# Three query transposes of a two-layer hybrid attention trunk: from TensorE to 32x32 squares on VectorE and SBUF-to-SBUF transfers

## What is computed

```python
h = rms_norm(x, pre_w)
dq, dk, dv, dg, sq, sk, sv, sg, iq, ik, iw = split(h @ w_in)
dq, dk = rope(dq), rope(dk)                    # 4 heads x 2 maps x 64
oa = diff_attention(dq, dk, dv, lam)           # scale 64 ** -0.5
sq, sk = rope(sq), rope(sk)                    # 4 heads x 128
iq, ik = rope(iq), rope(layer_norm(ik))        # 8 index heads x 64
score = sum_h relu(iq_h @ ik.T) * iw_h         # the 64 best keys of each query are kept
ob = softmax over kept keys(sq @ sk.T * 128 ** -0.5) @ sv
y = concat(rms_norm(oa) * silu(dg), ob * silu(sg)) @ w_out
x = x + rms_norm(y, post_w)
```

## Time and profile before

| | us |
|---|---|
| median of three runs | 312.75 (311.55 to 312.98) |
| profiled execution, whole | 313.99 |
| its span, first to last instruction | 312.2 |
| PE busy in the span | 302.6 (97%) |
| DVE busy | 237.6 (76%) |
| ACT busy | 164.7 (53%) |
| POOL busy | 69.4 (22%) |
| packets of the hardware DMA queue, share of 16 engines | 48.2% |

### The profile page before, as it was taken

One profiled execution on the slowest core, in us unless ns is written; L12 is line 12 of the kernel. 1 busy time (PEld: TensorE's weight loads), 2 busy tenths in 40 slices (PEclk: granted clock), 3 DMA queues, 4 the chain that ended last, 5 costly groups with the idle time before them and its releaser, 6 DMA issues.

```text
span 312.2 us, 4324 instructions
## 1 busy us (share of the span) xinstructions
PE 302.6 (97%) x1564; PEld 250.2 (80%) x1564; DVE 237.6 (76%) x483; ACT 164.7 (53%) x284; POOL 69.4 (22%) x107
## 2 busy tenths in 40 slices
PE   8889999999999999999999999999999999999992
PEld 7668887787887888888888888778878788888881
DVE  4663979699999996883995178969999999679243
ACT  4678844736576275601775375463747635561100
POOL 1278910025030501101051301003413050110001
PEclk9999999999999999999999999999999999999998
DMA  7999969234514358134038576834452326300011
GB/s 233 361 346 351 364 230 327 81 133 146 198 61 138 121 190 316 49 133 134 0 112 290 171 242 260 278 129 134 134 161 110 135 71 205 129 2 0 0 67 67
DMA packets 27556, 51.61 MB, mean 165 GB/s; under 512 B 3344, under 2 KB 3600, under 8 KB 27536
## 3 DMA queue, kind: packets, MB, share of 16 engines
q1 hardware_dynamic: 27536, 51.34, 48.2%
HBM read 50.29 MB, written 1.05 MB: 164 GB/s over the span
## 4 chain that ended last, share of the span: by engine, by line
PE 91%; DMA 4%; SPq 2%; DVE 1%; ACT 1%; issue 0%; DVEq 0%; POOLq 0%; POOL 0%; ACTq 0%
PE bank_a L380 19%; PE bank_a L389 19%; PE bank_a L385 19%; PE bank_a L534 7%; PE bank_s L534 7%; PE bank_t L359 6%; DMA w_raw<-in_w_in 4%; PE bank_o L514 3%; PE bank_a L457 2%; PE bank_s L497 2%; PE bank_s L489 1%; PE bank_s L477 1%; PE bank_s L389 1%; PE bank_s L380 1%; PE bank_s L385 1%; SPq L283 1%
## 5 line engine op out<-in xcount | busy, mean ns | idle before, releaser
L870 DVE TENSOR_TENSOR w_lo<-w_raw,w_hi 128x2048 fp32r<-128x2048 f32 (+1 forms) x46 | 99.2, 2164 | 23.3 <-ACT w_hi L669 23.2
L669 ACT ACTIVATE w_hi<-w_raw 128x2048 fp32r<-128x2048 f32 (+1 forms) x46 | 82.0, 1785 | 39.8 <-PE bank_a L389 34.3
L380 PE MATMUL bank_a<-w_hi,h_hi 128*128 128x512 f32 x256 | 72.1, 403 | 0.0
L389 PE MATMUL bank_a<-w_lo,h_hi 128*128 128x512 f32 x256 | 68.8, 390 | 0.0
L385 PE MATMUL bank_a<-w_hi,h_lo 128*128 128x512 f32 x256 | 68.6, 390 | 0.0
L385 PEld LDWEIGHTS bank_a<-w_hi,h_lo 128*128 128x128 f32 x256 | 48.1, 188 | 10.4
L389 PEld LDWEIGHTS bank_a<-w_lo,h_hi 128*128 128x128 f32 x256 | 47.9, 188 | 10.5 <-DVE w_lo L870 0.5
L380 PEld LDWEIGHTS bank_a<-w_hi,h_hi 128*128 128x128 f32 x256 | 45.5, 188 | 10.2 <-issue 2.6
L1272 POOL TENSOR_TENSOR rt<-nat,tab 128x256 f32<-128x256 f32 x10 | 7.4, 736 | 110.7 <-ACT nat L714 110.6
L730 ACT ACTIVATE xt_pbuf<-xt_pbuf,st 128x128 f32<-128x128 f32 (+1 forms) x48 | 21.3, 445 | 12.7 <-DVE st L997 12.4
L714 ACT ACTIVATE nat<-bank_a,st 128x512 f32<-128x512 f32 x20 | 13.7, 684 | 23.3 <-PE bank_a L389 22.1
(11 more groups left out here) (174 smaller groups left out, 447.0 us busy)
## 6 DMA issues: line engine op xcount, KB each, us to landing
w_raw<-in_w_in SPq DMA_DIRECT2D x34, 1024.0 KB, 5.2
w_raw<-in_w_out SPq DMA_DIRECT2D x8, 1024.0 KB, 5.1
w_raw<-in_w_in SPq DMA_DIRECT2D x4, 512.0 KB, 6.7
prm<-in_rows SPq DMA_DIRECT2D x2, 705.0 KB, 8.9
xres<-in_x SPq DMA_DIRECT2D x2, 512.0 KB, 13.2
out<-xres SPq DMA_DIRECT2D x4, 256.0 KB, 2.1
xt_pbuf<-in_x_t SPq DMA_DIRECT2D x3, 256.0 KB, 6.3
w_raw<-in_w_in SPq DMA_DIRECT2D x4, 144.0 KB, 6.3
```

The source lines that it names most:

```text
L380: pe.matmul(bank, h_hi[:, HALF * half + kk, tok], whi[:, kk, :], start=half == 0 and kk == 0, stop=False)
L389: mm = pe.matmul(bank, h_hi[:, HALF * half + kk, tok], wlo[:, kk, :], start=False, stop=half == 1 and kk == HALF - 1)
L669: act.activation(unit(w_hi, u), unit(raw, u), ACT.Copy).then_inc(hi_done.sem, 1)
L870: dve.tensor_tensor(unit(w_lo, u), unit(raw, u), unit(w_hi, u).bitcast(F32), ALU.subtract).then_inc(lo_done.sem, 1)
```

## The change

`turn_nat` is no longer called for IQ, DQ and SQ; it stays for DK and SK. In its place:

- DVE turns all of a `nat` slot (both blocks, 128x1024) into 32x32 squares, each transposed in its own place, in one instruction that writes `mixn` (called `squares`).
- SP moves the squares: for each pair (i, j) of four row and four column groups one transfer from partitions 32i to 32i+31 to partitions 32j to 32j+31, of 32x8x32 float32, so 16 transfers of 32 KB in runs of 128 bytes. They are written into SP's program behind the load that follows `split_lo` of units 7, 12 and 15, after a wait for `squares_done`.
- PE waits for `iq_landed`, `dq_landed`, `sq_landed` before the score matmuls. DVE waits for the earlier spread before it writes `squares` again.
- DVE's drains for the three go. The scales of DQ and SQ, which the drains applied, move into ACT's `move`: POOL computes two more scaled copies of `rx` for each block (`rd`, `rs`).
- The layout of `iqT`, `dqT`, `sqT` is by block, then by 128-column group. The uses of the T banks fall from 25 to 19.

```diff
+SPREAD_BEHIND = (7, 12, 15)
+            def spread(dst, landed):
+                for i in range(SQUARES):
+                    for j in range(SQUARES):
+                        src = squares[i * LANES:(i + 1) * LANES, :].rearrange("p (a j r) -> p a j r", j=SQUARES, r=LANES)[:, :, j, :]
+                        to = dst[j * LANES:(j + 1) * LANES, :, :, i * LANES:(i + 1) * LANES].rearrange("p b f r -> p (b f) r")
+                        sp.dma_start(to, src).then_inc(landed.sem, 16)
...
+                    if u == SPREAD_BEHIND[0]:
+                        sp.wait_ge(squares_done.sem, squares_done.at(layer, 1))
+                        spread(iqT, iq_landed)
...
                 second(6)
-                turn_nat(T_IQ, 0, 1)
                 first(7)
...
                 pe.wait_ge(t_drained.sem, t_drained.at(layer, T_IK + 1))
+                pe.wait_ge(iq_landed.sem, iq_landed.at(layer, iq_landed.per_layer))
                 index_logits(0, 0, range(4))
...
                 first(11)
-                turn_nat(T_DQ, 1, 2)
                 second(11)
...
                 second(14)
-                turn_nat(T_SQ, 1, 4)
                 first(15)
...
+                    if chunk in (DQ, SQ):
+                        act.wait_ge(rq_ready.sem, rq_ready.at(layer, b + 1))
+                    if chunk in (DK, SQ):
+                        act.wait_ge(squares_done.sem, squares_done.at(layer, 1 if chunk == DK else 2))
+                    root = {DQ: rd, SQ: rs}.get(chunk, rx)
...
+                def turn_squares(slot, rope):
+                    dve.wait_ge(rope_done.sem, rope_done.at(layer, rope))
+                    if rope == 2:
+                        dve.wait_ge(iq_landed.sem, iq_landed.at(layer, iq_landed.per_layer))
+                    if rope == 4:
+                        dve.wait_ge(dq_landed.sem, dq_landed.at(layer, dq_landed.per_layer))
+                    dve.transpose(squares, nat[:, slot, :, :].rearrange("p b n -> p (b n)")).then_inc(squares_done.sem, 1)
...
                 split_lo(layer, 7)
+                turn_squares(0, 1)
                 split_lo(layer, 8)
                 index_key()
-                drain_pair(T_IQ, iqT)
...
                 choose(0, 4)
+                turn_squares(1, 2)
                 split_lo(layer, 13)
                 choose(0, 4)
                 mask_unchosen(0)
-                drain_pair(T_DQ, dqT, DIFF_QK ** -0.5)
...
+                turn_squares(1, 4)
                 split_lo(layer, 16)
-                drain_pair(T_SQ, sqT, E ** -0.5)
...
+                pool.wait_ge(rx_ready.sem, rx_ready.at(layer, b + 1))
+                pool.tensor_scalar(rd[:, b:b + 1], rx[:, b:b + 1], DIFF_QK ** -0.5, None, ALU.mult)
+                pool.tensor_scalar(rs[:, b:b + 1], rx[:, b:b + 1], E ** -0.5, None, ALU.mult).then_inc(rq_ready.sem, 1)
```

More of the change, by code:

```diff
@@ L80 @@
 ROW_N = sum(ROW.values())
-T_IQ, T_IK, T_DQ, T_DK, T_SQ, T_PD0, T_PD1A = 4, 6, 7, 9, 11, 13, 14
-T_SK, T_PD1B, T_MD0, T_PS0, T_MD1, T_PS1A, T_PS1B, T_MS0, T_MS1 = 15, 17, 18, 19, 20, 21, 22, 23, 24
-T_USES = 25
+T_IK, T_DK, T_PD0, T_PD1A, T_SK, T_PD1B = 4, 5, 7, 8, 9, 11
+T_MD0, T_PS0, T_MD1, T_PS1A, T_PS1B, T_MS0, T_MS1 = 12, 13, 14, 15, 16, 17, 18
+T_USES = 19
+LANES = 32
+SQUARES = P // LANES
 S_IDX, S_DIFF0, S_DIFF1, S_DSA0, S_DSA1 = 0, 6, 8, 12, 13
@@ L131, in build_trunk @@
         ik2 = sb("ik2", [P, BLOCKS, 2, IDX_DIM])
-        iqT = sb("iqT", [P, HEADS, SEQ])
+        iqT = sb("iqT", [P, BLOCKS, HEADS, P])
         ikT = sb("ikT", [P, SEQ])
-        dqT = sb("dqT", [P, HEADS, SEQ])
+        dqT = sb("dqT", [P, BLOCKS, HEADS, P])
         dkT = sb("dkT", [P, HEADS, SEQ])
-        sqT = sb("sqT", [P, HEADS, SEQ])
-        skT = iqT
+        sqT = sb("sqT", [P, BLOCKS, HEADS, P])
+        skT = iqT[:, :, :, :].rearrange("p b f t -> p (b f t)").rearrange("p (f s) -> p f s", f=HEADS)
         xt = sb("xt_pbuf", [P, XT_N])
@@ L166, in build_trunk @@
         subln = st[:, 152:153]
+        rd, rs = st[:, 154:156], st[:, 156:158]
+        squares = mixn[:, :, :].rearrange("p b n -> p (b n)")
         A = [pb("bank_a0", [P, WIDTH]), pb("bank_a1", [P, WIDTH])]
@@ L200, in build_trunk @@
         out_landed = sem("out_landed")
-        t_filled = count("t_filled", T_USES, -T_IQ)
-        t_drained = count("t_drained", T_USES, -T_IQ)
+        t_filled = count("t_filled", T_USES, -T_IK)
+        t_drained = count("t_drained", T_USES, -T_IK)
         s_filled = count("s_filled", S_USES)
@@ L220, in build_trunk @@
         rope_done = count("rope_done", 5)
+        squares_done = count("squares_done", 3)
+        iq_landed = count("iq_landed", 16 * SQUARES ** 2)
+        dq_landed = count("dq_landed", 16 * SQUARES ** 2)
+        sq_landed = count("sq_landed", 16 * SQUARES ** 2)
+        rq_ready = count("rq_ready", BLOCKS)
         subln_ready = count("subln_ready", 1)
@@ L305, in _ @@
                     sp.dma_start(unit(raw, u + RING), weights(layer, u + RING)).then_inc(raw_landed[u % RING].sem, 16)
+                    if u == SPREAD_BEHIND[0]:
+                        sp.wait_ge(squares_done.sem, squares_done.at(layer, 1))
+                        spread(iqT, iq_landed)
+                    if u == SPREAD_BEHIND[1]:
+                        sp.wait_ge(squares_done.sem, squares_done.at(layer, 2))
+                        spread(dqT, dq_landed)
+                    if u == SPREAD_BEHIND[2]:
+                        sp.wait_ge(squares_done.sem, squares_done.at(layer, 3))
+                        spread(sqT, sq_landed)
                 if layer < DEPTH - 1:
@@ L337, in bank_t @@
                 def bank_t(j):
-                    if layer or j >= T_IQ + 2:
+                    if layer or j >= T_IK + 2:
                         pe.wait_ge(t_drained.sem, t_drained.at(layer, j - 1))
@@ L476, in index_logits @@
                             rows_h = slice(IDX_DIM * odd, IDX_DIM * (odd + 1))
-                            mm = pe.matmul(banks[odd][:, i * n:(i + 1) * n], iqT[rows_h, pair, b * P:(b + 1) * P],
+                            mm = pe.matmul(banks[odd][:, i * n:(i + 1) * n], iqT[rows_h, b, pair, :],
                                            ikT[rows_h, 0:n], start=True, stop=True)
@@ L488, in diff_scores @@
                             rows_m = slice(DIFF_QK * m, DIFF_QK * (m + 1))
-                            mm = pe.matmul(banks[m][:, i * n:(i + 1) * n], dqT[rows_m, h, b * P:(b + 1) * P],
+                            mm = pe.matmul(banks[m][:, i * n:(i + 1) * n], dqT[rows_m, b, h, :],
                                            dkT[rows_m, h, 0:n], start=True, stop=True)
@@ L496, in dsa_scores @@
                     for i, h in enumerate(heads):
-                        mm = pe.matmul(bank[:, i * n:(i + 1) * n], sqT[:, h, b * P:(b + 1) * P],
+                        mm = pe.matmul(bank[:, i * n:(i + 1) * n], sqT[:, b, h, :],
                                        skT[:, h, 0:n], start=True, stop=True)
@@ L578, in body @@
                 pe.wait_ge(t_drained.sem, t_drained.at(layer, T_DK + 2))
+                pe.wait_ge(dq_landed.sem, dq_landed.at(layer, dq_landed.per_layer))
                 diff_scores(6, 0, range(HEADS))
@@ L602, in body @@
                 pe.wait_ge(t_drained.sem, t_drained.at(layer, T_SK + 2))
+                pe.wait_ge(sq_landed.sem, sq_landed.at(layer, sq_landed.per_layer))
                 dsa_scores(12, 0, range(HEADS))
@@ L713, in move @@
                         act.wait_ge(rx_ready.sem, rx_ready.at(layer, b + 1))
+                    if chunk in (DQ, SQ):
[3 more added lines that the diff above has]
+                    root = {DQ: rd, SQ: rs}.get(chunk, rx)
                     act.activation(dst, bank_of(layer, g)[:, 0:width], ACT.Silu if chunk in (DG, SG) else ACT.Copy,
-                                   scale=rx[:, b:b + 1]).then_inc(proj_moved.sem, 1)
+                                   scale=root[:, b:b + 1]).then_inc(proj_moved.sem, 1)
                 def relu(j):
```

## The result

The changed kernel takes **316.9 us** (median of 4 runs, 315.18 to 317.94), the kernel before in the same session 312.87 (311.55 to 313.25). The ratio is 1.0117, with a 95% interval of 1.0089 to 1.0145: 4 us slower, where 2 us faster was forecast. The profiled execution took 317.94 us, with a span of 316.1, so 3.9 us more than the 314.0 of before. Ratios here leave out executions over 1.5% above a kernel's fastest; where a version ranges widely (e9, e12), its median and range over all executions are given as well.

What follows compares the result with a forecast made beforehand. PE, busy 97%, bounds the kernel, with DVE pacing one stretch. -2.9 us for two layers and +0.6 for the first layer's index key give -2.3: 310.5 us against 312.75, 8-in-10 range 308.5 to 317.

Steps and rivals of the forecast that it cites:

- the price of a transfer: SP's sixteen issues for each spread: 0.47 us each, between bounds of 0.42 and 2.3.
- the point of loss: Issue price per spread transfer from which the changed kernel is slower than before: 0.59 us.
- rival 1: SP's queue holds the spread's burst: each 0.1 us over costs 1.6 us a layer; slower, to over 335 us; chance 0.32.
- The landing: First spread, from SP's last issue until the data has landed: 1.7 us.
- The transpose: DVE's one-instruction transpose of 128x1024 float32: 1.2 us, replacing drains of the same time.
- Rival 2: DVE's transpose needs two passes, 1.1 us more each: +3.2 us, 316 us; chance 0.09.
- The index key of the first layer: PE stalls 0.6 to 0.7 us before its transpose, as DVE waits for POOL's later rotation; +0.6 us in the sum.
- What PE keeps: Of 3.0 us a layer freed on PE, 1.45 us survive; the rest becomes waits, with about 1.8 us before unit 17.
- DVE is 95% busy: DVE, busy 40.87 of 43.1 us from 58.9 on, sets the pace there and limits what PE keeps.
- Rival 3: DVE's stretch has unseen slack, for instance POOL's 2.67 us turning into 0.74: up to 3.0 us a layer kept, 307 to 309; chance 0.08.
- The bytes: A spread's 4096 runs of 128 bytes at 20 ns: 5.1 us on the transfer engines, hidden under 7.5 us of issuing.
- Second and third spread: Both land before PE's logits want them: the second with 3.7 us of slack, the third with twice that.

Runs made afterwards that it cites:

- e9: e5 with DVE's transpose of the index query moved behind unit 8's subtraction and POOL's four scalings behind the rotation: median 313.85 us, 310.61 to 316.51.
- e12: e9 with DVE's subtraction for unit 17 moved ahead of the last selection round, the masking and a copy: median 313.82 us, 309.22 to 315.73.
- e3: Changed kernel with each spread transfer in 1 KB runs instead of 128-byte runs, data landing in the wrong order: 315.35 us, ratio 1.0059.
- e4: Kernel before with sixteen unneeded 32 KB transfers in SP's idle time, in four forms of run length, source and partitions: 313.16 us in one run.
- e14: Changed kernel with SP waiting for the first spread's landing before it issues the next weights: 317.5 us, ratio 1.014.
- e15: e9 with SP waiting for the first spread's landing before it issues the next weights: 310.63 us, ratio 0.9939.
- e7: Changed kernel with index queries back on TensorE, less two selection rounds for the second block (1.96 us of DVE): 313.13 us, ratio 0.9996.
- e10: Changed kernel with index queries back on TensorE, unit 17's subtraction moved ahead of the last selection round, masking and a copy: 312.0 us, ratio 0.9978.
- e5: Changed kernel with eight of the first spread's sixteen transfers issued by ACT and eight by SP: 313.5 us, ratio 0.9998.
- e13: e12 with SP waiting for the first spread's landing before it issues the next weights: 309.99 us, ratio 0.9905.

## Why the prediction was wrong

- **The step that failed is the price of a transfer.** The forecast took 0.47 us from 0.42 (a single issue) and 0.555 (the opening burst) "because these transfers carry 32 KB and only one load is ahead". They cost 0.66 and 0.72 us (10.55 / 16 and 11.55 / 16), and neither longer runs nor another source would have changed that much (e3, e4). Both rows that the price came from are of other transfers. The reason given for the low end was wrong: 32 KB are not cheaper to issue than 1 MB, they took 0.61 us where a weight load took 0.37, from the first transfer of a burst on. The 0.72 holds one issue of 1.77 us; e14's second burst, without one, took 10.41 us, and PE waited 1.03 us there instead of 2.16. The text had set the point of loss at 0.59. By rival 1's own rule, from 0.48 and 0.56 on, 0.66 and 0.72 give 16 x 0.18 + 16 x 0.16 = 5.4 us, and 310.5 + 5.4 = 315.9, against 316.9 measured. Its waits of PE were found: 2.74 us in the first layer and 2.16 in the second. Rival 1 had the right term and the right place, at a chance that the opening burst's 0.555 should have made larger. Its mechanism was not what the rows show: it expected a full queue that slows issuing as the burst goes on, and the last issue of the first burst took 0.61 us like the third. That 0.555 lies near 0.61 is luck, as far as the runs show.
- **A term was missing**: the fall of PE's clock behind a wait, 1.6 us in the profiled execution, though not in every one. The prediction counted waits at their length only.
- **The landing**: 1.7 us after the last issue was forecast; 2.0 from its start, 1.4 from its end, were measured.
- **The transpose**: 1.2 us forecast, 1.24 measured. Rival 2 fell. The index key of the first layer: 0.6 forecast, 0.73 measured at the weight load, for the reason given (POOL's rotation ended at 37.97, forecast 38.1).
- **What PE keeps** of its 3.0 us: 1.45 us a layer forecast. Measured 0.9 x 3 - 1.25 = 1.45. e15 shows it whole: its profile stands at -1.32 us at the first row of the table above and at -3.33 at the last, which is 2.0 us for five of the six transposed chunks, and with 0.9 for the first one 2.9 us, as forecast. Its times are 2.6 us below the kernel before by the medians, 1.9 by the ratio. The wait for unit 17 was 1.47 us (1.8 forecast).
- **Its reason was half right.** "DVE is 95% busy" does not mean that DVE paces the whole stretch: from the masks at 83 to 87 us its selection rounds stood beside ACT's exponentials (e7). From there on DVE paces (e10), but POOL's rotation stands 1 us behind it, which the prediction had put on the same chain without its own price. Rival 3 had named POOL's 2.67 us, though as a gain.
- **The bytes**: hidden, as forecast; e3 puts the short runs at 1.5 us at most. Late weights: ACT waits 3.7 us for a load of `w_out` in each layer (in the first it had waited 2.92 us for PE at that place before), and PE does not wait for it. Second and third spread: no wait, as forecast. They take 11.2 to 11.7 us each. The second's slack of 3.7 us is used up: its last transfer is issued at 82.4 and takes 2.0 us to land, and the logits start at 84.66. The third had some 3.6 us left.

## What to carry to other kernels

Before work is traded for many small transfers, count the transfers and price each by an issue of the same kind. Here that was 0.6 to 0.7 us of the issuing engine; the 0.37 of a large weight load did not carry over, although it moves 32 times the bytes. If the trace has none of the kind, a handful of idle ones added to the kernel before (e4) gives the price for one run. Run length came second here. If a chain of transfers ends on the critical path, split it over two issuing engines and keep the next large load off the transfer engines until it has landed. And a busy share of 95% over a stretch doesn't name the pacing engine for each part of it: take work away at one place and look where the gap opens.

## What the runs showed of the hardware

- Issuing 32 KB transfers took 0.59 to 0.64 us each by the median, from HBM and SBUF alike, the first of a burst after 9.7 us without an issue 0.59, while loads of 705 KB and 1 MB took 0.34 to 0.37 us when issued by themselves (e4, after). Two sequencers did so side by side without slowing each other (5.37 and 5.38 us for eight each, e5). Five of the six bursts in the changed kernel's profile hold one issue of 1.4 to 1.8 us; ACT had one of 2.09 (e12).
- A 32 KB transfer whose issue took 2.09 us, while a load of 1 MB was issued on the other queue, landed 6.5 us after the start of its issue instead of 2.0 (e12); with the loads held back, one of 1.99 us landed after 3.4 (e13).
- A DVE transpose of 128x1024 float32 in 32x32 squares took 1.24 us, the same as a subtraction of that many elements.
- The granted clock fell to its lower level for about 3 us after PE waits of 2.2 to 3.1 us in some executions and not in others (2.76 us in e14: no fall).
- An operation of POOL of 0.74 us took 2.7 us beside DVE's subtraction of 2048 elements, be it the first of a rotation (e10) or the last.
